# Attention scores as two 64-row products in two PSUM banks, with the values' product moved to the head of each slot

## The reference, cut to what matters

```python
# layer 0, mixer B: 16 heads of 64; three dilated windows, mixed by their softmax denominators
q = apply_partial_rope(q) * 64 ** -0.5;  k = apply_partial_rope(k)
outs, lses = zip(*[dilated_branch(q, k, v, w, d) for w, d in ((128, 1), (512, 4), (2048, 16))])
y_b = sum(softmax(lses)[i] * outs[i] for i in range(3))

# layer 1: differential attention, 16 heads, each with two maps of 64 and values of 128
s = jnp.einsum('bqhje,bkhje->bhjqk', qblk, k)        # j = 0, 1: the two maps of a head
p = jax.nn.softmax(s, axis=-1)
att = p[:, :, 0] - lam * p[:, :, 1]
o = jnp.einsum('bhqk,bkhe->bqhe', att, v)            # then a norm per head
```

## Time and profile before

| | us |
|---|---|
| median of three runs | 2159.02 |
| the profiled execution's own time | 2158.62 |
| its span, first to last instruction | 2156.8 |
| PE busy | 2141.2 (99%) |
| DVE busy | 1698.2 (79%) |
| ACT busy | 1489.6 (69%) |
| score products, layer 0 (L1586), 64 records | 16.4 busy |
| score products, layer 1 (L1590), 64 records | 32.6 busy |
| values' products (L1614 and L1619), 256 records | 35.5 busy |

### The profile page before, as it was taken

One profiled execution on the slowest core, in us unless ns is written; L12 is line 12 of the kernel. 1 busy time (PEld: TensorE's weight loads), 2 busy tenths in 40 slices (PEclk: granted clock), 3 DMA queues, 4 the chain that ended last, 5 costly groups with the idle time before them and its releaser, 6 DMA issues.

```text
span 2156.8 us, 26554 instructions
## 1 busy us (share of the span) xinstructions
PE 2141.2 (99%) x9771; PEld 1765.4 (82%) x9771; DVE 1698.2 (79%) x1538; ACT 1489.6 (69%) x1774; POOL 230.7 (11%) x274
## 2 busy tenths in 40 slices
PE   9999999999999999999999999999999999999998
PEld 7888888888888888888887787788888888888886
DVE  5577466898898888888755656678998888888886
ACT  6677544787777777777655555447777777777774
POOL 0851000000000000000021001001000000000001
PEclk9999999999999999999999999999999999999999
DMA  9545445799989999997564454557999999998993
GB/s 315 189 154 194 145 148 198 255 290 298 266 256 263 282 296 276 285 289 230 183 215 146 149 169 143 177 175 239 278 299 273 275 292 279 281 292 266 263 263 149
DMA packets 226559, 508.82 MB, mean 236 GB/s; under 512 B 13736, under 2 KB 16384, under 8 KB 214656
## 3 DMA queue, kind: packets, MB, share of 16 engines
q1 hardware_dynamic: 214192, 422.68, 55.6%
q0 software_dynamic: 11520, 83.89, 19.7%
q10 hardware_dynamic: 720, 0.56, 0.1%
HBM read 416.92 MB, written 6.29 MB: 196 GB/s over the span
## 4 chain that ended last, share of the span: by engine, by line
PE 95%; DVE 2%; issue 1%; ACT 1%; DMA 1%; SPq 0%; ACTq 0%; POOLq 0%; POOL 0%; DVEq 0%
PE acc L1477 34%; PE acc L1696 20%; PE sc L1490 20%; PE pv L1490 10%; PE acc L1490 5%; PE tp L1504 3%; PE sc L1590 1%; DVE w_lo L1791 1%; PE pv L1619 1%; PE sc L1586 1%; PE pv L1614 1%; DMA raw<-in_ev_w_in 0%; PE sc L1569 0%; PE pv L1569 0%; ACT h_hi L1097 0%
## 5 line engine op out<-in xcount | busy, mean ns | idle before, releaser
L1791 DVE TENSOR_TENSOR w_lo<-raw,w_hi 128x2048 fp32r<-128x2048 f32 x263 | 601.6, 2293 | 100.2 <-PE acc L1477 41.5
L1051 ACT ACTIVATE w_hi<-raw 128x2048 fp32r<-128x2048 f32 x263 | 503.7, 1916 | 120.4 <-PE acc L1477 45.6
L1477 PE MATMUL acc<-w_hi,h_hi 128*128 128x512 f32 x936 | 261.4, 401 | 2.6 <-ACT h_hi L1021 2.6
L1477 PE MATMUL acc<-w_lo,h_hi 128*128 128x512 f32 x936 | 252.2, 391 | 0.2
L1477 PE MATMUL acc<-w_hi,h_lo 128*128 128x512 f32 x936 | 251.1, 390 | 0.0
L1791 DVE TENSOR_TENSOR w_lo<-xs,w_hi 128x2048 fp32r<-128x2048 f32 x88 | 201.2, 2288 | 31.3 <-PE acc L1696 20.4
L1477 PEld LDWEIGHTS acc<-w_lo,h_hi 128*128 128x128 f32 x936 | 175.6, 188 | 38.9 <-DVE w_lo L1791 1.4
L1477 PEld LDWEIGHTS acc<-w_hi,h_lo 128*128 128x128 f32 x936 | 175.5, 188 | 37.0
L1477 PEld LDWEIGHTS acc<-w_hi,h_hi 128*128 128x128 f32 x936 | 171.1, 189 | 37.0 <-issue 5.5
L1051 ACT ACTIVATE w_hi<-xs 128x2048 fp32r<-128x2048 f32 x88 | 168.5, 1915 | 23.9 <-PE acc L1490 8.1
L1317 ACT ACTIVATE yacc<-acc 128x512 f32<-128x512 f32 x160 | 95.0, 595 | 113.3 <-PE acc L1696 113.3
(11 more groups left out here) (299 smaller groups left out, 3615.6 us busy)
## 6 DMA issues: line engine op xcount, KB each, us to landing
raw<-in_od_w_in SPq DMA_DIRECT2D x48, 1024.0 KB, 5.1
raw<-in_ffn_w_gate SPq DMA_DIRECT2D x38, 1024.0 KB, 9.7
raw<-in_ev_w_in SPq DMA_DIRECT2D x37, 1024.0 KB, 5.3
raw<-in_ffn_w_up SPq DMA_DIRECT2D x36, 1024.0 KB, 7.8
raw<-in_ffn_w_down SPq DMA_DIRECT2D x36, 1024.0 KB, 6.6
xs<-in_ffn_w_up SPq DMA_DIRECT2D x22, 1024.0 KB, 8.0
xs<-in_ffn_w_down SPq DMA_DIRECT2D x18, 1024.0 KB, 7.2
xs<-in_ffn_w_gate SPq DMA_DIRECT2D x18, 1024.0 KB, 10.2
```

The costliest lines, as they stand in the source:

```text
L1051: act.activation(w_hi[u % HI][:, :, :], raw[place.buf][:, :, :], ACT.Copy).then_inc(hi_done, 1)
L1477: mm = pe.matmul(acc[n % 2][t][:, :], operand(lhs, a, k, t), w[:, k, :], start=first and k == 0 and j == 0, stop=last and k == KT - 1 and ...
L1791: dve.tensor_tensor(w_lo[u % LO][:, :, :], raw[plan.place[u].buf][:, :, :], w_hi[u % HI][:, :, :].bitcast(F32), ALU.subtract).then_inc(lo_ ...
```

## The change

Four things, in one diff. (1) Each score task is two products of 64 rows, one for each head or map (`m`), on the row half in which its queries and keys lie. (2) `sc` and `pv` become two parts of one tensor of two banks, `heads`; the scores of m = 0 go to the first half of the first bank, those of m = 1 to the second half of the second, and the values' results to the first half of the second. (3) A task of layer 0 is one half of the queries of two heads, no longer all queries of one head. (4) The order in a slot is `pv`, `pt`, `s0`, `s`. Two waits come with it: `s0` waits until every values' product that stands ahead of it in the list has been fetched (`o_done`, `task.m`), and `pv` until all scores ahead of it have been read.

```diff
-        for kind, lag in (("s0", 0), ("pt", 1), ("pv", 2), ("s", 0)):
+        for kind, lag in (("pv", 2), ("pt", 1), ("s0", 0), ("s", 0)):
@@ number
+        elif task.kind == "s0":
+            task.m = plan.products
+            plan.scores += 1
+        elif task.kind == "pv":
+            task.m = plan.scores
+            plan.products += 1
@@ trunk
-        sc = ctx.enter_context(nc.psum_tensor("sc", [P, 2, T], F32))
-        pv = ctx.enter_context(nc.psum_tensor("pv", [P, 2, T], F32))
+        heads = ctx.enter_context(nc.psum_tensor("heads", [P, 4, T], F32))
+        sc, pv = heads[:, 0:2, :], heads[:, 2:4, :]
+        scores = heads[:, 0::3, :]
@@ ACT softmax
-                    for t in range(NT):
-                        ins = act.activation(prob[:, t, :], prob[:, t, :], ACT.Exp, scale=SCALE, bias=nmx[:, t:t + 1],
-                                             accum_out=den[n % 2][:, t:t + 1])
+                    for m in range(2):
+                        ins = act.activation(prob[:, m, :], prob[:, m, :], ACT.Exp, scale=SCALE, bias=nmx[:, m:m + 1],
+                                             accum_out=den[n % 2][:, m:m + 1])
...
-                        ins = act.activation(prob[:, m, :], sc[:, m, :], ACT.Exp, scale=SCALE, bias=nmx[:, m:m + 1],
+                        ins = act.activation(prob[:, m, :], scores[:, m, :], ACT.Exp, scale=SCALE, bias=nmx[:, m:m + 1],
@@ PE, s0
+                    if task.m:
+                        pe.wait_ge(o_done, task.m)
...
-                    if task.layer == 0:
-                        for t in range(NT):
-                            mm = pe.matmul(sc[:, t, :], q[:, kt, t * P:(t + 1) * P], k[:, kt, task.i % 2, :],
-                                           start=True, stop=True)
-                    else:
-                        t = task.i % 2
-                        mm = pe.matmul(sc[:, :, :].rearrange("p m t -> p (m t)"), q[:, kt, t * P:(t + 1) * P],
-                                       k[:, kt, :, :].rearrange("p m t -> p (m t)"), start=True, stop=True)
+                    t = task.i % 2
+                    for m in range(2):
+                        rows = slice(m * HD, (m + 1) * HD)
+                        mm = pe.matmul(scores[:, m, :], q[rows, kt, t * P:(t + 1) * P], k[rows, kt, m, :],
+                                       start=True, stop=True)
@@ PE, pv
+                    if task.layer == 1:
+                        pe.wait_ge(exp_done, task.m)
+                    else:
+                        pe.wait_ge(s_free, task.m)
...
-                        for t in range(NT):
+                        for m in range(2):
+                            head = task.i // 2 * 2 + m
                             for j in range(2):
-                                mm = pe.matmul(pv[:, 0, t * HD:(t + 1) * HD], probT[:, j, t * P:(t + 1) * P],
-                                               v[:, j, task.i * HD:(task.i + 1) * HD], start=j == 0, stop=j == 1)
+                                mm = pe.matmul(pv[:, 0, m * HD:(m + 1) * HD], probT[:, j, m * P:(m + 1) * P],
+                                               v[:, j, head * HD:(head + 1) * HD], start=j == 0, stop=j == 1)
@@ DVE, softmax
-                    for t in range(NT):
-                        ins = dve.tensor_tensor_reduce(prob[:, t, :], sc[:, t, :], logc[:, t, :], 1.0, 3.0 * NEG,
-                                                       ALU.add, ALU.max, mx[:, t:t + 1])
+                    for m in range(2):
+                        ins = dve.tensor_tensor_reduce(prob[:, m, :], scores[:, m, :], logc[:, task.i % 2, :], 1.0, 3.0 * NEG,
+                                                       ALU.add, ALU.max, mx[:, m:m + 1])
...
-                    dve.tensor_reduce(mx, sc[:, :, :], AX.X, ALU.max).then_inc(max_part, 1)
+                    dve.tensor_reduce(mx, scores, AX.X, ALU.max).then_inc(max_part, 1)
@@ DVE, values of layer 0
-                        ins = dve.tensor_scalar(tok[:, t, task.i * HD:(task.i + 1) * HD], pv[:, 0, t * HD:(t + 1) * HD],
-                                                rden[:, t:t + 1], None, ALU.mult)
+                        ins = dve.tensor_scalar(tok[:, t, head * HD:(head + 1) * HD], pv[:, 0, m * HD:(m + 1) * HD],
+                                                rden[:, m:m + 1], None, ALU.mult)
```

More of the change, by code:

```diff
@@ L194, in __init__ @@
         self.stat, self.update, self.squared, self.y_gained = {}, {}, {}, {}
-        self.bodies = 0
+        self.bodies = self.scores = self.products = 0
         self.place, self.after, self.heads_of, self.head_units, self.x_read, self.wholes, self.last_body = {}, {}, [], [], [], {}, []
@@ L1596, in task_of @@
                         flat_tp = tp[task.e % 2][:, :, :].rearrange("p a b -> p (a b)")
-                        transposes(task.e, [(flat_tp[:, j * T + t * P:j * T + (t + 1) * P], prob[:, t, j * P:(j + 1) * P])
-                                            for j in range(2) for t in range(NT)])
+                        transposes(task.e, [(flat_tp[:, j * T + m * P:j * T + (m + 1) * P], prob[:, m, j * P:(j + 1) * P])
+                                            for j in range(2) for m in range(2)])
                     else:
```

## The result

| | us |
|---|---|
| before, median of six runs | 2159.01 (2158.26 to 2159.08) |
| after, median of six runs | 2172.9 (2171.38 to 2175.74) |
| ratio | 1.0066, 95% interval 1.0053 to 1.0078 |
| after, the profiled execution and its span | 2172.45 and 2170.6 |

The forecast was 2176.7 us, with 2171 to 2183 as its own range. Of 17.7 us forecast, 13.9 came.

A forecast was written before the change was run, and what follows sets the result against it. TensorE (PE), busy 99% of the span, was taken as the bound. Order and waits 5.0 + 5.3 + 4.6 - 2.6 = 12.3 us, plus 5.4 for height changes, gave +17.7: 2176.7 us, range 2171 to 2183, chance 0.42.

The forecast's parts named there:

- The order and its wait: Scores now wait for DVE's fetch of the values: +5.0 us in 18 slots, +5.3 in six, +4.6 in 12.
- four steps: Rival: the row halves do not overlap, so a task's scores stay at 0.86 us; 2187.2 us, chance 0.18.
- three steps: Score pair: only A-second and B-first overlap among four records, 0.64 us instead of 0.86, saving 0.22 a task.
- the rival of full pairs: Score halves run fully side by side in two steps, 0.43 us; 2166.5 us, or 2161.1 with free height changes; chance 0.16.
- The change of height: Switches between 128-row and 64-row products: 54 at 0.10 us each, 5.4 us in all; ends 0 and 14.6.
- The second rival: Three steps, but each switch between 128-row and 64-row products drains and reloads at 0.27 us; 2185.9 us, chance 0.16.
- The slots without the wait: 12 slots with scores whose awaited values are long fetched: they only gain, -0.22 us each, -2.6 us before height changes.
- the free edits: Values' product's other waits, ACT's square ahead of its copy, tasks of two heads, moved transpose stalls: all put at nothing.
- The last group: Second mixer's last six slots: the new wait closes a loop through DVE, 7.88 us instead of 7.00, +5.3 us in all.
- the other waits of the values' product: Its waits for the previous scores' exponentials (second mixer) or maximum (first) are met early and cost nothing.
- The stalls behind the transpose banks: Transposes waiting for copies out of their banks, 0.2 us in single slots: they move, but into the same wait.
- What I said PE's waits would show: In the profile after: waits for DVE's values' fetch, 24 and 12 times, 0.5 to 0.7 us, last group above 1.

The follow-up runs named there:

- e1: Changed kernel with order and both new waits kept, but each score product over all 128 rows, no 64-row products: 2181.57 us.
- e5: e4 with each pair of 64-row score products computed twice in a row into the same place: 2176.06 us.
- e6: e5 with one small full-height product between the two pairs, so the height changes twice more per task: 2203.63 us.
- e7: Changed kernel, but in the second mixer's output-projection slots DVE fetches the values before adding the second half of the output: 2170.52 us.
- e2: Changed kernel, 64-row pairs kept, with the values' product moved behind the first half of its slot: 2164.78 us.
- e4: e2 with the scores also put ahead of the transposes of the probabilities, 64-row pairs kept: 2157.31 us.
- e8: e4 with each score product over all 128 rows instead of 64-row pairs: 2160.15 us.

## Why the prediction was right, and where it was right for a wrong reason

- The order and its wait: right. They were priced at 9.0 + 6.6 + 7.2 = 22.8 us with four steps, and e1 measured 22.4, by its trace 21.9 of them in the 36 slots. The terms can be followed in the timeline after: the values' last record ends at 1174.76, the copy runs from 1174.80 to 1175.09, the weight load starts at 1175.21. Only the last 0.11 us isn't there as such: the first score record starts 0.03 us after its weight load, and the next pass follows after 0.29 us and not 0.215.
- The steps of a pair: wrong. "I take 0.64 us, three steps" rested on an order A-first, A-second, B-first, B-second, in which B-first could not start before A-second. The records start two by two, 0.007 us apart, and the second two follow after 0.32 us in the first pair and after 0.215 us in the next (e5). It is the rival of full pairs that was right here: a pair is two steps, 0.43 us. In which order the four stand in PE's queue the trace doesn't show.
- The change of height: mis-sized. 0.10 us was taken, 0.18 measured (e6). The upper bound was 0.27. The second rival had this direction. The reason for taking the low side, that switches between full-height products cost nothing, told nothing of a change of height.
- The two errors had opposite signs. Per task with the wait, three steps with one change at 0.10 are 0.74 us; two steps with one at 0.18 are 0.61, and the timeline after has 0.63 from the first score record to the projection's first. So the sum came out only 3.8 us too high, and that it came so near is in part luck. The slots without the wait are the clearest case: a gain of 0.22 less 0.20 was forecast, it was 0.43 less about 0.40, and the ten in which nothing else changed gave 0.2 us together, as forecast. With two steps and 0.18 us a change the forecast's own sum would have been 2.1 + 54 x 0.18 = 11.8 us, 2 under what came; the stalls named below under the free edits (0.5) and what came in before the first attention slot (0.4) are part of that, the rest is spread over the slots.
- The last group: mechanism right, size too high. The loop was forecast at 7.88 us with three steps and 7.67 with two; it is 7.60. e7 shows that the addition is in it.
- The free edits: the other waits of the values' product cost nothing, as forecast. The stalls behind the transpose banks were put at nothing and did not balance: one slot gained 0.40 us (the transposes of `tok` no longer wait), one lost 0.82 (probabilities behind `h_lo`, 1.1 us of waiting). Both are slots without the wait for the fetch, so it could not take the stall in.
- What I said PE's waits would show, 0.5 to 0.7 us each and 36 times, was wrong as a reading: they show mostly 0.26 in layer 1, 0.42 in layer 0 and 0.58 in the last group, 34 times. A wait is counted from the end of the last record and not from where the next could have started, and in two slots a transpose had waited before.

The Trainium skill (TensorE: Matmul & The Clock Gate, section Part 3: Packing small matmuls) gives about 4 ns between the starts of products in different row groups; e5's records say 7 ns. The prediction took three steps from its order of starts; the records show two. The page of the Trainium skill on tiling (TensorEngine Tiling (Array Packing), section Tiling Modes) says that a change of mode drains TensorE. e6's 0.18 us for each change fits that, but no run shows that a drain is what takes the time.

## What to carry to other kernels

Two half-height products side by side save PE time only if they save more than two changes of height cost. Here one pair of 256 float32 columns saved 0.43 us and paid about 0.37. In e5 a second pair right behind the first took 0.43 us and paid for no further change, so several pairs in a row should share the price; no run here replaces useful full-height work that way.

Before an order is turned so that a product waits for another engine's read of the previous product's bank, put the length of that hand-over beside what else PE could do meanwhile. Here the turned order cost 22.4 us by e1, nearly all of it in the 36 slots with the wait, more than the pairs gave back. Moving the earlier product half a slot ahead took the wait away but uncovered stalls behind the transpose banks (e2); it needed the scores ahead of the transposes too (e4). e4 is the one version under the kernel before, by 0.1%, with an interval that ends at 1.0, so it can't be told from no change.

## What the runs showed of the hardware that was not expected

- Two 64-row float32 products of 256 columns on different row halves take 0.43 us together (e5), as long as one full-height product of 256 columns (two records of 0.215 us in e8).
- In the changed kernel's timeline PE loads no weights for 0.33 us after the last 64-row weight load, then those of the next full-height product. Ahead of 64-row products the load waits too, here 0.17 us behind the transposes of a second slot:

```profile
206.03 0.30 PEld L1596 LDWEIGHTS heads<-gx,queries 64*128 64x128 f32 x4 [0.17 <-issue]
```

- After a wait or a change of height the first 64-row record starts 0 to 0.03 us after its weight load (1175.21 and 1175.24 above), and the next records come 0.29 to 0.32 us later, where the second pair of e5 has 0.215. The same shape stands in the kernel before without any change of height: behind the values' product the projection's weight load starts at 1170.37 and its first record at 1170.40. So I read the first record as beginning with its weight load, with no more than 0.215 us of work in it; that is a reading of the starts, not a measurement of its own.
